# Difference heads first, turned four at a time, and the output product begun before attention ends

## What is computed

```python
proj = h @ w_in                      # 1024 -> 2212 columns
# columns: c_q 384, c_kv 256, k_rope 32 | dq dk dv 256 each | fq fk fv 256 each | ff 4
q  = rms_norm(c_q) @ w_uq            # MLA: 8 heads, 64 + 32 rotated
kv = rms_norm(c_kv) @ w_ukv          # MLA: 8 heads, key 64 and value 64
o_mla  = attention(q, [kv_key, rope(k_rope)], kv_value)        # chunk-causal mask
o_diff = rms_norm((softmax(q1 k1) - lam * softmax(q2 k2)) v)   # 4 heads, q and k of width 32, v of 64
o_fox  = softmax(q k / 8 + cum_i - cum_j) v                    # 4 heads, forget gates summed over time
h = layer_norm(alpha * h + concat(o_mla, o_diff, o_fox) @ w_out)
h = layer_norm(alpha * h + grouped_moe(h))                     # 16 experts
```

## Time and profile before

| | |
|---|---|
| three runs | 1844.34 median, 1843.21 to 1847.57 us |
| the profiled execution | 1841.65 us, of this the span of the trace is 1839.9 us |
| TensorE busy (matmuls) | 1593.1 us, 87% |
| VectorE / ScalarE busy | 934.1 us (51%) / 629.4 us (34%) |
| granted TensorE clock, mean | 0.925 of full speed |
| attention layer 1 (the third layer), in the trace | from 939.8 us; its output product ends at 1102.9 us |
| attention layer 2 (the fourth layer) | its output product ends at 1553.4 us |

### The profile page before, as it was taken

How to read it: one execution, slowest core, us unless ns; L and a number is a source line. 1 busy time by engine, 2 the same in 40 slices (tenths; PEclk the granted TensorE clock), 3 DMA queues, 4 the chain that set the end, 5 groups by cost and what they waited for, 6 DMA issues and landing times.

```text
span 1839.9 us, 18878 instructions
## 1 busy us (share of the span) xinstructions
PE 1593.1 (87%) x7511; PEld 1099.6 (60%) x7511; DVE 934.1 (51%) x1338; ACT 629.4 (34%) x891; POOL 31.1 (2%) x62
## 2 busy tenths in 40 slices
PE   2889987999699986999968985999878896799985
PEld 1677766888587775788857863333327775433331
DVE  4896666755488665655375745111016584311002
ACT  2335534343334453444345631111114561211111
POOL 2000000000000000000030000000000000000000
PEclk9899998999899998999989986999998898799998
DMA  9686355956578434665463224999975124499994
GB/s 336 229 277 205 114 165 191 321 169 218 170 273 285 151 115 137 224 211 181 138 192 106 92 113 186 410 409 409 409 295 196 59 92 190 196 409 409 409 409 194
DMA packets 149963, 427.65 MB, mean 232 GB/s; under 512 B 8104, under 2 KB 16544, under 8 KB 149872
## 3 DMA queue, kind: packets, MB, share of 16 engines
q1 hardware_dynamic: 146192, 417.43, 62.0%
q0 software_dynamic: 3456, 8.87, 1.7%
q10 hardware_dynamic: 224, 0.07, 0.0%
HBM read 425.30 MB, written 1.05 MB: 232 GB/s over the span
## 4 chain that ended last, share of the span: by engine, by line
PE 44%; DVE 7%; SPq 6%; DMA 3%; ACT 2%; issue 2%; DVEq 0%
PE gp L2052 12%; PE gp L2395 8%; PE gp L2224 8%; SPq L709 6%; PE gp L2414 4%; PE mp L2435 2%; DMA raw_more<-in_exp_w_up 2%; PE gp L2380 2%; PE mp L2243 1%; PE mp L2264 1%; PE mp L2275 1%; PE mp L2274 1%; DVE stats L1598 1%; DVE wlo L1178 1%; PE mp L2283 1%
## 5 line engine op out<-in xcount | busy, mean ns | idle before, releaser
L1251 DVE TENSOR_TENSOR wlo<-raw,whi 128x2048 fp32r<-128x2048 f32 (+1 forms) x132 | 289.5, 2194 | 223.7 <-ACT whi L810 222.4
L810 ACT ACTIVATE whi<-raw 128x2048 fp32r<-128x2048 f32 (+1 forms) x132 | 242.1, 1835 | 365.7 <-PE gp L2052 209.5
L2052 PE MATMUL gp<-whi,xt_hi 128*128 128x512 f32 (+1 forms) x800 | 318.0, 398 | 31.4 <-DVE xt_lo L1300 14.1
L2052 PE MATMUL gp<-wlo,xt_hi 128*128 128x512 f32 (+1 forms) x800 | 311.7, 390 | 0.0
L2052 PE MATMUL gp<-whi,xt_lo 128*128 128x512 f32 (+1 forms) x800 | 311.6, 389 | 0.0
L2052 PEld LDWEIGHTS gp<-whi,xt_hi 128*128 128x128 f32 x800 | 155.0, 194 | 71.4 <-DVE wlo L1251 16.0
L2052 PEld LDWEIGHTS gp<-whi,xt_lo 128*128 128x128 f32 x800 | 154.5, 193 | 31.2
L2052 PEld LDWEIGHTS gp<-wlo,xt_hi 128*128 128x128 f32 x800 | 155.2, 194 | 29.3 <-issue 0.2
L1920 DVE TENSOR_SCALAR pr<-slots,key,dg 128x128 f32<-128x128 f32 x64 | 19.3, 344 | 260.6 <-PE gp L2425 260.6
L2224 PE MATMUL gp<-whi,xt_hi 128*128 128x512 f32 (+1 forms) x224 | 88.7, 396 | 8.8 <-DVE xt_lo L1643 6.0
L1178 DVE TENSOR_TENSOR wlo<-raw,whi 128x2048 fp32r<-128x2048 f32 (+3 forms) x36 | 68.5, 1906 | 42.1 <-ACT whi L956 41.6
(11 more groups left out here) (387 smaller groups left out, 2352.7 us busy)
## 6 DMA issues: line engine op xcount, KB each, us to landing
raw<-in_w_in SPq DMA_DIRECT2D x60, 1024.0 KB, 5.7
raw<-in_w_ada SPq DMA_DIRECT2D x42, 1024.0 KB, 5.3
raw_deep<-in_exp_w_down SPq DMA_DIRECT2D x36, 1024.0 KB, 16.9
raw_deep<-in_exp_w_gate SPq DMA_DIRECT2D x30, 1024.0 KB, 14.5
raw_deep<-in_exp_w_up SPq DMA_DIRECT2D x30, 1024.0 KB, 16.7
raw<-in_w_gate SPq DMA_DIRECT2D x20, 1024.0 KB, 5.2
raw<-in_w_up SPq DMA_DIRECT2D x20, 1024.0 KB, 5.2
raw<-in_w_down SPq DMA_DIRECT2D x20, 1024.0 KB, 4.9
```

Source lines behind the costliest of these rows:

```text
L810: act.activation(slot(whi, s % SPLIT, units, cols), slot(raw, g % RAW, units, cols), ACT.Copy).then_inc(hi_done.sem, 1)
L1251: dve.tensor_tensor(slot(wlo, s % SPLIT, units, cols), slot(raw, g % RAW, units, cols), slot(whi, s % SPLIT, units, cols).bitcast(F32), AL ...
L2052: mm = pe.matmul(gp[:, q % 2, t, 0:wide], a[:, chunk, ts], w[:, unit, c0:c0 + wide], start=first and n == 0 and m == 0, stop=last and n == ...
```

## The change

- The input projection's columns come in the order 2048, 0, 512, 1024, 1536. The latents are complete after unit 5. Their norm is taken behind unit 6 and they are turned behind unit 8, into the banks of `mp`.
- The jobs' order is difference heads (0 to 7), MLA heads (8 to 15), fox heads (16 to 19). No step stands beside the input projection: step 0 comes behind unit 9, steps 1 to 4 behind units 10 to 13, steps 5 to 20 alone.
- The queries of four difference halves (4 x 32 = 128 columns) are turned together, and so are their keys: `turn_qk` and the copy of line 982 are done in steps 0 and 4 only, for four jobs each. The scores of such a job read 32 rows of the turned block, at row 0, 32, 64 or 96. `TURNED` is 14 turns, where there were 20.
- `forget_gates(2)` loses the copies of fox queries and keys, which become `forget_gates(3)`, behind step 1 on VectorE. `shared_key` moves from unit 8 to unit 9.
- Units 14, 15 are now the first half of the sum (MLA heads) for both column groups, 16, 17 the second half. The first four chunks are turned after step 20 into two banks of `gp`; steps 21 and 22 follow, then unit 14, step 23, unit 15, the other four chunks, units 16 and 17.

```diff
-IN2_COLS = [(COLS * j, min(COLS, IN2 - COLS * j)) for j in reversed(range(IN2_JOBS))]
+IN2_COLS = [(COLS * j, min(COLS, IN2 - COLS * j)) for j in [IN2_JOBS - 1, *range(IN2_JOBS - 1)]]
-JOBS = [MH + 2 * DH + i for i in range(FH)] + [MH + i for i in range(2 * DH)] + list(range(MH))
-FIRST_DIFF, FIRST_MLA = FH, FH + 2 * DH
+JOBS = [MH + i for i in range(2 * DH)] + list(range(MH)) + [MH + 2 * DH + i for i in range(FH)]
+FIRST_DIFF, FIRST_MLA, FIRST_FOX = 0, 2 * DH, 2 * DH + MH
+TOGETHER = P // DW
+def turn_of(i):
+    return i // TOGETHER if i < FIRST_MLA else i - FIRST_MLA + 2 * DH // TOGETHER
+BETWEEN = S2_OUT - S2_UQ + 1
@@ ScalarE
-                if s >= S2_UQ - IN_STEPS:
-                    attend(s - (S2_UQ - IN_STEPS))
...
+                if s == 6:
+                    for t in range(NT):
+                        act.activation(rt1[:, 0:CQ], pr[:, t, 0:CQ], ACT.Square, accum_out=lsum4[:, t:t + 1]).then_inc(mla_sq.sem, 1)
...
+                    act.wait_ge(*rv2_ready.at2(l, 1))
+                    act.activation(rs[:, 0:4], rv[:, 0:4], ACT.Sqrt).then_inc(rs2_ready.sem, 1)
+                if s == 8:
+                    for b in range(3):
+                        n = 2 if b < 2 else 1
+                        high(mp[:, b, :], X2_MLA + b, mt_hi[:, 2 * b:2 * b + n, :], n)
+            attend(0)
             for s in range(S2_UQ, S2_OUT):
...
+                attend(s - S2_UQ + 1)
+            for i in range(BETWEEN, AJ + 1):
+                attend(i)
+            for b in range(2):
+                high(out_banks[b], X2_O + b, xt_hi[:, 2 * b:2 * b + 2, :])
+            for i in range(AJ + 1, AJ + 4):
+                attend(i)
@@ VectorE
+                if s == 6:
+                    dve.wait_ge(*mla_sq.at2(l, 4))
...
+                    reciprocal_root(4, rs2_ready.at2(l, 1), lk)
+                    for t in range(NT):
+                        for i, (a, b) in enumerate(((0, CQ), (CQ, CQ + CKV))):
+                            lk(dve.scalar_tensor_tensor(out=pr[:, t, a:b], in0=pr[:, t, a:b], scalar=rr[:, 2 * i + t:2 * i + t + 1],
...
+                    dve.sem_inc(mla_ready.sem, 1)
                 if s == 7:
                     rotate_diff()
                 if s == 8:
+                    spread(X2_MLA, (2, 2, 1), (mt_hi, mt_lo), turned_banks)
+                if s == 9:
                     shared_key()
...
+            spread(X2_O, (2, 2), (xt_hi, xt_lo), out_banks)
+            attend(AJ + 1)
+            attend(AJ + 2)
+            split2(S2_OUT + 2, l)
+            attend(AJ + 3)
             difference(3)
+            split2(S2_OUT + 3, l)
+            spread(X2_O, (2, 2), (xt_hi, xt_lo), out_banks, 2)
@@ TensorE
             def turn_qk(j):
+                if FIRST_DIFF <= j < FIRST_MLA:
+                    c = P * (turn_of(j) - FIRST_DIFF)
+                    q, k = pr[:, :, C_DQ + c:C_DQ + c + P], pr[:, :, C_DK + c:C_DK + c + P]
             def scores(j):
+                r = DW * ((j - FIRST_DIFF) % TOGETHER) if FIRST_DIFF <= j < FIRST_MLA else 0
-                qk = qkt[0:w, j % 2, :]
+                qk = qkt[r:r + w, turn_of(j) % 2, :]
...
+                if s == 8:
+                    pe.wait_ge(*mla_ready.at2(l, 1))
+                    for b in range(3):
+                        turn(mp[:, b, :], pr, 2 * P * b, 2 if b < 2 else 1)
+            attend(0)
             for s in range(S2_UQ, S2_OUT):
                 product(s)
+                attend(s - S2_UQ + 1)
+            for i in range(BETWEEN, AJ + 1):
+                attend(i)
+            for b in range(2):
+                turn(out_banks[b], oa, 2 * P * b).then_inc(tr_done.sem, 1)
+            attend(AJ + 1)
+            attend(AJ + 2)
+            pe.wait_ge(*ft_lo.at2(l, X2_O + 2))
+            product(S2_OUT)
+            attend(AJ + 3)
+            product(S2_OUT + 1)
+            pe.wait_ge(*oa_ready.at2(l, 1))
+            for b in range(2, 4):
+                turn(out_banks[b], oa, 2 * P * b).then_inc(tr_done.sem, 1)
+            product(S2_OUT + 2)
+            product(S2_OUT + 3)
```

More of the change, by code:

```diff
@@ L643, in program @@
         small = bank_tr
-        latent_banks = (gp[:, 1, 0, :], gp[:, 1, 1, :], gp[:, 0, 0, :])
+        turned_banks = [mp[:, b, :] for b in range(4)]
+        out_banks = [gp[:, 0, 0, :], gp[:, 0, 1, :], mp[:, 2, :], mp[:, 3, :]]
         first_banks = (bank_xg, bank_tr, bank_y, bank_gu, bank_xg, bank_tr, bank_y, bank_xg)
@@ L1832, in _ @@
                         difference(i - (FIRST_MLA + 4))
-                spread(X2_O, (2, 2), (xt_hi, xt_lo), turned_banks)
-                difference(3)
[L1835 to L1847, removed]
+                spread(X2_O, (2, 2), (xt_hi, xt_lo), out_banks)
[3 more added lines that the diff above has]
+                attend(AJ + 3)
+                difference(3)
+                split2(S2_OUT + 3, l)
+                spread(X2_O, (2, 2), (xt_hi, xt_lo), out_banks, 2)
+                for n in range(2):
+                    q = J2_OUT + n
+                    dve.wait_ge(*w_used.at2(l, job2_end(q) + 1))
+                    xs = x[:, :, COLS * n:COLS * (n + 1)]
+                    dve.scalar_tensor_tensor(out=xs, in0=xs, scalar=ALPHA, in1=gp[:, q % 2, :, :], op0=ALU.mult, op1=ALU.add).then_inc(x2_sum.sem, 1)
+                    dve.wait_ge(*x2_sum.at2(l, n + 1))
+                    dve.sem_inc(pair_free[q % 2].sem, 2)
                 layer_norm(x, rs2_ready.at2(l, 3), lnw_in.at2(l, 32), lk, True)
@@ L2298, in attend @@
                         scores(i - 1)
[L2299 removed]
+                    if turned_here(i):
                         turn_qk(i)
@@ L2316, in _ @@
                         pe.matmul(mp[:, 3, FH:2 * FH], tri[:, :], fz[:, 1, :], start=False, stop=True).then_inc(cum_done.sem, 1)
-                    if s >= S2_UQ - IN_STEPS:
-                        attend(s - (S2_UQ - IN_STEPS))
-                for i in range(IN_STEPS, NORM_STEPS):
-                    attend(i)
-                pe.wait_ge(*mla_ready.at2(l, 1))
-                for b in range(3):
-                    turn(latent_banks[b], pr, 2 * P * b, 2 if b < 2 else 1).then_inc(tr_done.sem, 1)
@@ L2325, in _ @@
-                attend(NORM_STEPS)
+                    if s == 8:
+                        pe.wait_ge(*mla_ready.at2(l, 1))
+                        for b in range(3):
+                            turn(mp[:, b, :], pr, 2 * P * b, 2 if b < 2 else 1).then_inc(tr_done.sem, 1)
                 pe.wait_ge(*ft_lo.at2(l, X2_MLA + 3))
+                attend(0)
                 for s in range(S2_UQ, S2_OUT):
                     product(s)
-                    attend(NORM_STEPS + 1 + s - S2_UQ)
-                for i in range(NORM_STEPS + 1 + S2_OUT - S2_UQ, AJ + 4):
+                    attend(s - S2_UQ + 1)
@@ L2331, in _ @@
+                for i in range(BETWEEN, AJ + 1):
                     attend(i)
-                pe.wait_ge(*o2_taken.at2(l, AJ))
-                for b in range(2):
-                    turn(mp[:, b, :], oa, 2 * P * b).then_inc(tr_done.sem, 1)
-                for s in range(S2_OUT, S2_MOE):
-                    if s < S2_OUT + 2:
-                        pe.wait_ge(*ft_lo.at2(l, X2_O + 2 * (s - S2_OUT) + 2))
-                    product(s)
-                    if s == S2_OUT:
-                        pe.wait_ge(*oa_ready.at2(l, 1))
-                        for b in range(2, 4):
-                            turn(mp[:, b, :], oa, 2 * P * b).then_inc(tr_done.sem, 1)
+                pe.wait_ge(*pair_free[0].at2(l, 10))
@@ new lines, in _ @@
+                pe.wait_ge(*o2_taken.at2(l, FIRST_FOX))
+                for b in range(2):
[7 more added lines that the diff above has]
+                pe.wait_ge(*oa_ready.at2(l, 1))
+                pe.wait_ge(*o2_taken.at2(l, AJ))
+                for b in range(2, 4):
+                    turn(out_banks[b], oa, 2 * P * b).then_inc(tr_done.sem, 1)
```

99 lines of the change are left out of this document (39 added, 60 removed).

## The result

| | before | changed |
|---|---|---|
| median of 4 runs each, us | 1845.95 (1843.21 to 1848.53) | 1819.09 (1812.33 to 1822.29) |
| ratio | | 0.985, 95% interval 0.9817 to 0.9882 |
| profiled execution, us | 1841.65 | 1822.29 |
| third layer, first projection matmul to the end of `w_out` | 943.17 to 1102.92: 159.8 | 952.23 to 1097.97: 145.7 |
| fourth layer, the same | 1388.48 to 1553.42: 164.9 | 1382.23 to 1533.53: 151.3 |

The kernel got 1.5% faster, 26.9 us by the medians, where 40.5 were forecast. The two changed stretches lose 14.0 and 13.6 us, 27.6 together, so the result is accounted for by them. The two profiled executions differ by only 19.4, because in the second one the third layer began 9.1 us later, behind two layers whose code is the same.

The account below looks back on a forecast made before the run. TensorE, busy 87% of the span, was taken as the bound. A new path of 88.2 us saves 19.7 and 20.8, together 40.5: profiled 1801.1, plus 2.7 for the median, 1803.8 us; range for 8 in 10, 1793 to 1819.

Parts of the forecast that it names:

- 1, unit 9 ends earlier by: Input projection: pieces of steps 0 to 2 leave (2.64 us), ten latent transposes enter (1.1); unit 9 ends 1.54 earlier.
- 2, the gap (inside 3): Between unit 9 and unit 10: 22.2 us become one turn of query and key, 0.45.
- 3, unit 9's end to step 5: Beside units 10 to 13: VectorE's queue sets the length, 20.6 us, where the same stretch took 23.2 before.
- 4, steps 5 to the last scores: Sixteen steps alone, about 2.3 us each, plus difference work, last scores and a low-clock stretch: 37.5 us, against 21.4 before.
- 5, the end: After the last scores to unit 17's end, at full clock: 30.1 us against 39.6 before.
- turning by fours: Steps 5 to 7: TensorE saves 0.44 us each, but waiting for VectorE's maxima keeps the loop at 2.3, so worth nothing.
- The rival that it does not: At the experts: if their weights and not the path hold them, no gain is left, 1844 us; chance 0.04.
- 1.3 for a stretch at low clock after the waits of part 3, as before: Bare steps from step 5: 1.7 us lost to half clock in the kernel before, some taken as hidden, so 1.3.
- One of the prediction's own signs of being wrong: Steps standing alone: the prediction is wrong if they take over 2.6 us each.
- The first rival: Clock falls in unit 14 (3.1 us) and a step or two alone (about 3.4) a layer: 1817 us; chance 0.17.
- The slow rival: From step 5 to unit 17 TensorE stays at 1.2 GHz, 42.3 us a layer: 1886 us; chance 0.03.

Follow-up runs that it names:

- e9: The changed kernel with the latents' norm and turning done behind unit 9, without their cover: ratio 1.0026, 1850.01 us.
- e11: e1 with VectorE and ScalarE work moved, four added matmuls before steps 4 and 5 each, and two score banks: ratio 0.9786.
- e6: The changed kernel with difference scores on all 128 rows from row 0, results wrong, for timing only: ratio 0.9819, 1808.87 us.
- e1: The changed kernel plus identity matmuls: five before step 4, six before step 5, two behind each of steps 5 to 7: ratio 0.9785, 1800.42 us.
- e2: The changed kernel with each difference half turned in its own step again, scores from row 0: ratio 0.9907, 1821.01 us.
- e5: The changed kernel plus only two 128 x 128 identity matmuls behind each of steps 5, 6 and 7: ratio 0.9876.

## Why the prediction was right and where not

The direction was right, and the time came out at the upper edge of the wide range: 1819.09 us for 1793 to 1819, where 1803.8 was forecast. The narrow range of 1797 to 1811, which had 0.66, was missed. By the steps of the prediction, third / fourth layer:

| part | predicted | measured | |
|---|---|---|---|
| 1, unit 9 ends earlier by | 1.54 | 2.3 / 1.7 | transposes 1.09, as forecast |
| 2, the gap (inside 3) | 0.45 | 0.44 | right |
| 3, unit 9's end to step 5 | 20.6 | 20.9 / 20.9 | right |
| 4, steps 5 to the last scores | 37.5 | 42.8 / 43.6 | wrong by 5.3 / 6.1 |
| 5, the end | 30.1 | 31.0 / 31.0 | 0.9 short |
| sum of 3 to 5 | 88.2 | 94.7 / 95.5 | |

**What was right.** The latents' chain is hidden beside units 6 to 8, and e9 shows that this is what the change stands on: uncovered, it costs 12 to 14 us a layer. VectorE ended part 3, and its queue was full as forecast (busy 18.92 of 20.90), at 20.9; that the chain spends 4.7 us of it on ScalarE was not in the account. The end came out at full clock, though other kernels with the same end show that this was not safe (e11). In bare steps at full clock turning by fours is worth nothing, as e6's step of 2.28 without a turn shows. That the gain reaches the end was right: from one layer's `w_out` to the next layer's first matmul it takes 284.3 us for 285.6. The rival that it does not had 0.04 and was wrong.

**What failed.** It is the term "1.3 for a stretch at low clock after the waits of part 3, as before" in part 4. It measured about 6.6 (1.3 and the 5.3 of the table), nearly all in steps 5 to 8, 15.3 us for 9.1. The prediction had the fall in the right place and took its length from a stretch of the kernel before in which MLA heads' scores ran. A better row lay at hand: the low-clock step of the earlier trace rows has 32-row scores, and from it on the clock stayed low for 10.5 us with TensorE busy (in the third layer for less). One of the prediction's own signs of being wrong came true: the fifteen periods of the third layer's bare steps average 2.79 us, over the 2.6 that it names, because of these four. The first rival had the mechanism, with 3.4 a layer for it in part 4 and a further 3.1 for unit 14 that did not come. That its 1817 nearly met the time is luck: one term was too small by what the other had too much. The slow rival's low clock over the whole bare stretch did occur, over four steps of the sixteen. The argument against it, that the steps from 1048 to 1063 ran at full clock, compared steps with 96-row scores to steps with 32-row ones. e6 (128 rows for 32) shows that this makes the difference, and e1 what the fall costs: 5.7 us a layer. The change's own order exposed the stretch: with difference heads first, the four bare steps with 32-row scores stand right behind the two waits.

**Turning by fours** is a smaller part that the prediction had at zero: e2 gives about 5 us in all by the medians and up to 9 by its trace. Part of it lies in the steps that ran at the low clock, where TensorE's own work is the bound (2.0 us a layer). As much lies beside units 10 to 13, where the prediction did not look for it, since there it saves turns and ScalarE's copies on the chain.

**What stays open.** Which property of the work the clock goes by. Busy time alone is not it (e2, e5). The scores' rows matter, or the values in them (e6), and two 128 x 128 matmuls of the identity a step hold the clock but do not bring it back (e1, e5). The identity is mostly zeros, and no run varies that. The Trainium skill (TensorE: Matmul & The Clock Gate, Part 4) says that transposes don't count as busy in the same way. e2's added transposes, 17.23 of 17.30 us busy at 0.50, agree with it but do not single it out: e5's added matmuls are no transposes, and with them TensorE was busy 13.48 of 13.50 us at 0.50 as well, while the MLA steps with their transposes held the full clock. Why unit 14 begins at the low clock in some traces is open too.

## What to carry to other kernels

Take the length of a low-clock stretch only from rows with the same work in it; here steps with 32-row scores took 3.7 us where such with 128-row scores took 2.3, though TensorE was the busier in the slow ones. Where the narrow work stands behind waits, fill them: here 17 throwaway matmuls a layer (11 in the waits, 6 in the steps behind them) bought 0.9%. Where independent work can be reordered, an order with the narrow matmuls (32 rows) beside a product and the wide ones alone is worth a try; no run here has it. And hide the serial chain first: the latents' norm moved beside a product is worth 12 to 14 us a layer here, more than any other part.

## What was not expected of the hardware

- TensorE busy 15.30 of 15.30 us at a granted clock of 0.50, for four steps, in both layers and, to 0.03 us, in both profiles of the changed kernel; with 128-row scores in the same places (e6) the clock is back after 3.5 us.
- Two 128 x 128 identity matmuls a step keep a clock that has not fallen at 1.00 (e1, steps of 2.42 to 2.44 us), and leave a fallen one at 0.50 (e5, 4.52).
- Two scores matmuls on 32 rows directly behind a product take 0.41 us before the second form begins, and the product behind them 3.33; on 128 rows (e6) 0.22 and 3.15. The first fence is the changed kernel's chain of waits, the second e6's.

```profile
1006.82 0.41 PE mp L2298 x2
1007.24 0.43 PE mp L2299 x2
1007.67 3.33 PE gp L2244 x18
```

```profile
999.11 0.22 PE mp L2298 x2
999.33 0.43 PE mp L2299 x2
999.76 3.15 PE gp L2244 x18
```

That is 0.37 us more for each time that scores on 32 rows stand between two products. The Trainium skill (TensorEngine Tiling (Array Packing), Key Properties) says that changing the tiling mode drains TensorE; these rows agree. The kernel before had it too (at step 8 0.41, and 0.54 for the turn behind it where the earlier trace rows has 0.45 for four), so it is hardly a part of the result.
